# Even projection steps, Q ahead of the norm's rates, and K's and V's low weight halves on GpSimd, in a two-layer decoder step

## What is computed

```python
u = rmsnorm(h, mix_norm[0])                   # x * rsqrt(mean(x*x) + eps) * gain
q, k, v = split(u @ w_qkv, 3)                 # 8 heads, each with two sub-heads of 128; v has 256
o = (softmax1 - lam * softmax2) @ v           # causal, with linear biases; lam from four vectors
h = h + (rmsnorm(o) * (1 - lam0)) @ w_o       # norm over each head's 256
h = h + (silu(g) * up) @ w_down               # g, up from rmsnorm(h) @ w_gate_up
# layer 1: trailing-window means and w_pool in place of attention, then the same SwiGLU
```

## Time and profile before

| | |
|---|---|
| median of 3 runs | 3268.26 us (3264.95 to 3281.38) |
| profiled execution | 3269.89 us, its span 3268.1 us |
| TensorE busy | 3123.6 us, 96% of the span |
| TensorE weight loads, beside the matmuls | 2922.0 us, 89% |
| DVE busy | 1557.7 us, 48% |
| ACT busy | 1062.5 us, 33% |
| POOL busy | 159.4 us, 5% |
| read from HBM | 625.37 MB |
| start of the page steps, end of the last score | about 227 us, 1128 us |

### The profile page before, as it was taken

How to read it: one execution, slowest core, us unless ns; L and a number is a source line. 1 busy time by engine, 2 the same in 40 slices (tenths; PEclk the granted TensorE clock), 3 DMA queues, 4 the chain that set the end, 5 groups by cost and what they waited for, 6 DMA issues and landing times.

```text
span 3268.1 us, 59382 instructions
## 1 busy us (share of the span) xinstructions
PE 3123.6 (96%) x25401; PEld 2922.0 (89%) x25401; DVE 1557.7 (48%) x2212; ACT 1062.5 (33%) x1509; POOL 159.4 (5%) x185
## 2 busy tenths in 40 slices
PE   5899999999998899999999999999999999999999
PEld 5887777777775589999999999999999999999999
DVE  3244444444444455444444444445645445444445
ACT  3123333333333343322222222224432332323333
POOL 1000000000000011000000000002200000000002
PEclk8999999999999999999999999999999999999999
DMA  5438999999989955443444444443444444444442
GB/s 151 135 127 302 345 337 338 331 338 338 340 326 334 338 168 170 141 142 131 151 134 148 136 145 139 144 141 103 137 155 152 145 155 143 154 148 150 152 145 97
DMA packets 341938, 637.98 MB, mean 195 GB/s; under 512 B 11528, under 2 KB 257775, under 8 KB 308367
## 3 DMA queue, kind: packets, MB, share of 16 engines
q1 hardware_dynamic: 337120, 620.67, 54.7%
q0 software_dynamic: 3328, 11.24, 1.0%
q10 hardware_dynamic: 1230, 2.29, 0.2%
HBM read 625.37 MB, written 9.23 MB: 194 GB/s over the span
## 4 chain that ended last, share of the span: by engine, by line
PE 86%; DVE 6%; ACT 4%; issue 3%; DMA 1%; POOL 0%; ACTq 0%; DVEq 0%; SPq 0%
PE ps L1640 71%; PE ps L1754 6%; PE ps L1799 3%; PE ps L1776 2%; DVE halves L1087 2%; ACT kv_hi L836 1%; ACT halves L789 1%; DVE keyT L1257 1%; PE ps L1898 1%; DMA raw<-in_cache_k_dram 1%; PE ps L1878 1%; PE ps L1789 1%; PE ps L2041 1%; ACT pa_s L920 0%; PE ps L2018 0%
## 5 line engine op out<-in xcount | busy, mean ns | idle before, releaser
L1087 DVE TENSOR_TENSOR halves<-raw,halves 128x2048 fp32r<-128x2048 f32 x300 | 687.1, 2292 | 629.0 <-ACT halves L789 628.9
L1640 PE MATMUL ps<-xhi,halves 128*128 128x320 f32 (+1 forms) x3840 | 873.9, 314 | 33.9 <-DVE halves L1087 31.8
L789 ACT ACTIVATE halves<-raw 128x2048 fp32r<-128x2048 f32 x300 | 573.3, 1911 | 893.7 <-PE ps L1640 888.4
L1640 PEld LDWEIGHTS ps<-xhi,halves 128*128 128x128 f32 x3840 | 657.5, 190 | 37.1 <-issue 34.9
L1640 PE MATMUL ps<-yhi,halves 128*128 128x336 f32 x2816 | 657.2, 317 | 0.1
L1640 PE MATMUL ps<-xlo,halves 128*128 128x320 f32 (+1 forms) x1920 | 602.3, 314 | 0.0
L1640 PEld LDWEIGHTS ps<-yhi,halves 128*128 128x128 f32 x2816 | 483.1, 188 | 0.5 <-issue 0.4
L1640 PE MATMUL ps<-ylo,halves 128*128 128x336 f32 x1408 | 447.1, 318 | 0.0
L1640 PE MATMUL ps<-hA_hi,halves 128*128 128x336 f32 (+1 forms) x1408 | 375.5, 314 | 3.0 <-DVE hT L1531 2.9
L1640 PE MATMUL ps<-hB_hi,halves 128*128 128x336 f32 (+1 forms) x1408 | 372.8, 312 | 0.0
L1640 PEld LDWEIGHTS ps<-xlo,halves 128*128 128x128 f32 x1920 | 366.1, 191 | 0.1
(11 more groups left out here) (216 smaller groups left out, 2866.7 us busy)
## 6 DMA issues: line engine op xcount, KB each, us to landing
raw<-in_w_gate_up_dram SPq DMA_DIRECT2D x176, 1024.0 KB, 5.1
raw<-in_cache_k_dram SPq DMA_DIRECT2D x128, 1024.0 KB, 6.5
raw<-in_cache_v_dram SPq DMA_DIRECT2D x128, 1024.0 KB, 8.0
raw<-in_w_down_dram SPq DMA_DIRECT2D x88, 1024.0 KB, 5.0
kv_raw<-in_w_qkv_dram SPq DMA_DIRECT2D x64, 512.0 KB, 7.9
raw<-in_w_qkv_dram SPq DMA_DIRECT2D x16, 1024.0 KB, 5.9
raw<-in_w_o_dram SPq DMA_DIRECT2D x16, 1024.0 KB, 5.4
raw<-in_w_pool_dram SPq DMA_DIRECT2D x4, 1024.0 KB, 5.5
```

What stands on the lines that cost most here:

```text
L789: act.activation(whi[t][:, :], raw[r][:, :], ACT.Copy).then_inc(hi_ready[t], 1)
L1087: dve.tensor_tensor(wlo[t][:, :], raw[r][:, :], whi[t][:, :].bitcast(F32), ALU.subtract)\
L1640: mm = pe.matmul(out, l, r, start=first and n == 0, stop=last and n == 2)
```

## The change

A head's projection takes 16 steps: two chunks in each, eight steps for K and eight for V, and a block is turned in the step in which the next one begins. The tile's plan is tied to those 16 steps and its last phase has a step of its own. All chunks of the input are turned ahead of Q's first block. The sum of squares is taken on ACT from the rows as they came (six squares of 1024 columns with an accumulated sum), POOL raises it to the power of -1/2, DVE multiplies the identity by it, and three products with ones spread it over the partitions; the square root, the reciprocal and the Newton step are gone. Only the gain of the first norm is loaded ahead; the rest follows behind Q's first block. DVE's low half of unit n+1 stands ahead of the copy of the block that unit n ends. In the page steps the low halves of K's and V's weights are made on POOL, and ACT makes the high half right behind the key copies. The engines' order within a step is changed, the new keys take one step each from 114 on, and from key page 116 on there are two more page slots, where x's low and high halves stood. POOL loads x again at step 113.

The diff, cut (renamed banks, places and semaphores are left out):

```diff
@@ -59,9 +59,7 @@
 KV_RAW, KV_HI = 3, 2
-KV_STEPS = 15
-K_QUOTA = (3, 3, 2, 2, 2, 2, 2, 0)
-V_QUOTA = (3, 3, 3, 3, 2, 2, 0)
+KV_STEPS = 16
@@ -69,15 +67,11 @@
     for h in range(1, H):
-        t = KV_STEPS * (h - 1)
-        for block, quota in ((2 * h, K_QUOTA), (2 * h + 1, V_QUOTA)):
-            c = 0
-            for n in quota:
-                chunks[t] = [(block, c + i) for i in range(n)]
-                c += n
-                if n == 0:
-                    ends[t] = block
-                t += 1
+        for i in range(2):
+            t = KV_STEPS * (h - 1) + 8 * i
+            for n in range(8):
+                chunks[t + n] = [(2 * h + i, 2 * n), (2 * h + i, 2 * n + 1)]
+            ends[t + 8] = 2 * h + i
@@ -87,8 +81,8 @@
 NEW_SEQ = (7, 0, 1, 2, 3, 4, 5, 6)
-NEW_AT = {106 + 2 * n: n for n in range(NB)}
-PAIR_AT = {122 + 2 * p: p for p in range(3)}
+NEW_AT = {114 + n: n for n in range(NB)}
+PAIR_AT = {124 + 2 * p: p for p in range(3)}
@@ -118,14 +112,32 @@
 PAGE_ORDER = page_order()
-PAGE_LOAD = {what: n for n, what in enumerate(x for x in PAGE_ORDER if x[0] != "w")}
+IN_STEPS = [x for x in PAGE_ORDER if x[0] != "w"]
+PAGE_LOAD = {what: n for n, what in enumerate(IN_STEPS)}
+MORE_FROM = PAGE_LOAD["k", KV_STEPS * (H - 1) + 4]
+def page_slots():
+    last, turns, out = {i: None for i in range(4)}, {i: 0 for i in range(SLOTS)}, []
+    for n in range(len(IN_STEPS)):
+        if n == MORE_FROM:
+            last.update({4: None, 5: None})
+        slot = min(last, key=lambda i: -1 if last[i] is None else last[i])
+        out.append((slot, turns[slot], last[slot]))
+        last[slot], turns[slot] = n, turns[slot] + 1
+    return out
+PAGE_SLOT = page_slots()
...
 FREE_USES = [
-    ("in", {3: 1, 4: 5, 5: 5, 6: 4, 7: 4}),
+    ("in", {3: 2, 4: 5, 5: 5, 6: 4, 7: 4}),
...
     ("qg", {b: 4 for b in range(4)}),
-    ("hx", {4: 8, 5: 8}),
+    ("hx", {4: 16}),
@@ -608,17 +625,19 @@
                     continue
-                slot = n % SLOTS
-                if n < RAW:
-                    half_slot, half_turn = nth(U_Q + 12 + n, SPLIT)
+                slot, _, had = PAGE_SLOT[n]
+                if had is not None:
+                    page_used(had)
+                elif slot < RAW:
+                    half_slot, half_turn = nth(U_Q + 12 + slot, SPLIT)
...
                 else:
-                    page_used(n - SLOTS)
+                    sp.wait_ge(kv_used, 4 * KV_BLOCKS)
...
             for j in range(RAW):
-                page_used(max(n for n in range(len(in_steps)) if n % SLOTS == j))
+                page_used(max(n for n in range(len(IN_STEPS)) if PAGE_SLOT[n][0] == j))
@@ -666,12 +685,9 @@
-            for c in range(1, DC):
-                pool.wait_ge(squares, squares_n(0, c))
-                if c > 1:
-                    pool.wait_ge(sums, sums_n(0, c - 1))
-                pool.tensor_tensor(acc0[:, :], sq0[:, 0, :] if c == 1 else acc0[:, :], sq0[:, c, :], ALU.add)\
-                    .then_inc(sums, 1)
+            pool.wait_ge(ms0_step, 2)
+            pool.wait_ge(ones_set, 3)
+            pow_half(rt0[:, :], ms0[:, :], half[:, 0:3]).then_inc(rt0_set, 1)
@@ -694,15 +710,25 @@
+            def kv_split_lo(n):
+                pool.wait_ge(kv_split, n)
+                pool.wait_ge(kv_hi_set, n + 1)
+                pool.tensor_tensor(kv_lo[n % KV_RAW][:, :], kv_raw[n % KV_RAW][:, :],
+                                   kv_hi[n % KV_HI][:, :].bitcast(F32), ALU.subtract).then_inc(kv_split, 1)
...
             for t in range(STEPS + 2):
+                for n in range(9, 4 * KV_BLOCKS):
+                    if KV_FIRST[n - 1] == t:
+                        kv_split_lo(n)
...
                     pow_half(prs, pms, half[:, 0:1]).then_inc(pa_rs, 1)
-                if t - 1 in KV_END:
-                    block_rows(KV_END[t - 1])
+                if t in KV_END:
+                    block_rows(KV_END[t])
@@ -793,15 +819,22 @@
                 act.activation(xhi[:, c, :], ps[b][:, 0:T], ACT.Copy, scale=gain_of(0, c)).then_inc(norm_hi, 1)
-                act.activation(sq0[:, c, :], ps[b][:, 0:T], ACT.Square).then_inc(squares, 1)
...
                     split_hi(U_Q + 1)
+            act.wait_ge(ss0_clear, 1)
+            for part in range(2):
+                for tile in range(3):
+                    r = ROWS[tile]
+                    if part:
+                        act.wait_ge(ss0_set, tile + 1)
+                    act.activation(junk0[tile][0:r, :], io_tm[0:r, tile, 1024 * part:1024 * part + 1024], ACT.Square,
+                                   accum_out=ss0[0:r, part, tile:tile + 1]).then_inc(ss0_set, 1)
+            for n in range(2, 4):
+                split_hi(U_Q + n)
...
             act.activation(lsc[0:1, 2:4], lsc[0:1, 0:2], ACT.Exp).then_inc(lam_exp, 1)
-            act.wait_ge(bank_free[7], bank_n("n0", 7, 0) + 1)
-            act.activation(r0[:, :], mean0[:, :], ACT.Sqrt).then_inc(rms_ready, 1)
@@ -949,19 +982,23 @@
             for t in range(-1, STEPS):
-                if t - 1 in KV_END:
-                    kv_rows(KV_END[t - 1])
+                if t + 1 < PAGES:
+                    keys_out(t + 1, 0)
+                if tile_at(t, 4) is not None:
+                    tile_squares(tile_at(t, 4))
+                if t + 1 < PAGES:
+                    keys_out(t + 1, 2)
+                if t in KV_END:
+                    kv_rows(KV_END[t])
+                for n in range(9, 4 * KV_BLOCKS):
+                    if KV_FIRST[n - 1] == t:
+                        kv_split_hi(n)
...
                     tile_turned(tile_at(t, 3))
-                if tile_at(t, 4) is not None:
-                    tile_squares(tile_at(t, 4))
-                if tile_at(t - PHASES, 0) is not None:
-                    tile_features(tile_at(t - PHASES, 0))
+                if tile_at(t, 5) is not None:
+                    tile_features(tile_at(t, 5))
...
                     out_features(PAIR_AT[t - 2])
-                if t + 1 < PAGES:
-                    keys_out(t + 1, 0)
-                    keys_out(t + 1, 2)
@@ -973,9 +1010,6 @@
                     tile_exps(tile_at(t, 1))
-                for n in range(9, 4 * KV_BLOCKS):
-                    if KV_FIRST[n - 1] == t:
-                        kv_split_hi(n)
@@ -1088,13 +1122,13 @@
+            dve.memset(ss0[:, :, :], 0.0).then_inc(ss0_clear, 1)
             dve.wait_ge(bank_full[3], 1)
-            dve.tensor_scalar(gains[:, :], ps[3][:, 0:96], 1.0, None, ALU.mult).then_inc(bank_free[3], 1)
+            dve.tensor_scalar(gains[:, 0:16], ps[3][:, 0:16], 1.0, None, ALU.mult).then_inc(bank_free[3], 1)
...
                 dve.wait_ge(norm_hi, c + 1)
-                dve.wait_ge(squares, squares_n(0, c))
@@ -1103,6 +1137,21 @@
+            dve.wait_ge(ss0_set, 6)
+            dve.tensor_tensor(ms0[:, :], ss0[:, 0, :], ss0[:, 1, :], ALU.add).then_inc(ms0_step, 1)
+            dve.wait_ge(ms0_step, 1)
+            dve.tensor_scalar(ms0[:, :], ms0[:, :], 1.0 / D, 1e-6, ALU.mult, ALU.add).then_inc(ms0_step, 1)
+            dve.wait_ge(rt0_set, 1)
+            for tile in range(3):
+                dve.tensor_scalar(diag0[tile][:, :], ident, rt0[:, tile:tile + 1], None, ALU.mult).then_inc(diag_set, 1)
+            split_lo(U_Q + 2)
+            dve.wait_ge(bank_full[7], bank_n("n0", 7, 0, True))
+            dve.tensor_scalar(r0[:, :], ps[7][:, 0:T], 1.0, None, ALU.mult).then_inc(bank_free[7], 1)
+            dve.wait_ge(bank_free[7], bank_n("n0", 7, 0) + 1)
+            dve.wait_ge(bank_full[3], 2)
+            dve.tensor_scalar(gains[:, 16:96], ps[3][:, 0:80], 1.0, None, ALU.mult).then_inc(bank_free[3], 1)
+            split_lo(U_Q + 3)
@@ -1136,8 +1191,6 @@
-            rates("n0", mean0[:, :], r0[:, :], newton0[:, :], 0, 0)
@@ -1212,18 +1265,16 @@
-            dve.wait_ge(consts_in, 16)
-            dve.tensor_scalar(crow0, sel[:, 1:2], lam_b, None, ALU.mult).then_inc(sign_step, 1)
-            dve.wait_ge(sign_step, 1)
-            dve.tensor_tensor(rowsign, crow0, sel[:, 0:1], ALU.add).then_inc(sign_step, 1)
             for n in range(1, 16):
-                if n > 1:
-                    split_lo(U_Q + n)
-                if n == 15:
+                if 3 <= n < 15:
+                    split_lo(U_Q + n + 1)
+                elif n == 15:
...
                     q_evac(n)
+                if n == 5:
+                    lambdas()
@@ -1420,9 +1471,6 @@
                     tile_join(tile_at(t, 2))
-                for n in range(9, 4 * KV_BLOCKS):
-                    if KV_FIRST[n - 1] == t:
-                        kv_split_lo(n)
@@ -1670,31 +1718,33 @@
-            for c in range(4):
+            for c in range(DC):
                 turn_in(c)
-            def input_ready(cc):
-                if cc + 4 < DC:
-                    turn_in(cc + 4)
-                pe.wait_ge(*chunk_done(0, cc))
...
                 take("qg", e, 0)
-            fm_block(U_Q, 0, 0, (0, 1), input_ready, 0)
```

(60 more changed lines are left out.)

107 lines of the change are left out of this document (59 added, 48 removed).

## The result

The changed kernel takes 3189.84 us (median of 4 runs, 3186.87 to 3191.74) against 3267.91 us before (4 runs, 3264.95 to 3281.38): a ratio of 0.9752, 95% interval 0.9724 to 0.9781. The forecast was 3204 us. The profiled execution took 3186.87 us, 83.0 less than the one of before, where the sum had -64. So the total came out near, but two of its terms did not, and they were off in opposite directions; that they cancelled in part is luck.

A forecast was written before the change was run, and what follows sets the result against it. TensorE was taken as the nearer limit in the page steps, DMA close, with TensorE waiting for low halves in Q. 3269.9 - 44 - 16 + 8 - 12 = 3206, stated as 3204 for the median; range 3185 to 3222.

The forecast's parts named there:

- Part 1: Q ahead of the page steps: TensorE's pauses for low halves go and block 0 ends earlier, a gain of 44 us.
- Part 2: Page steps with a projection: a 16-step cycle takes 109.8 us; -16 us over seven cycles, between -35 and 0.
- The port term: Page steps: GpSimd's low halves hold VectorE instructions with two SBUF inputs through the shared port, +8 us, bounds 0 and +40.
- two or three meetings per cycle: Page steps: VectorE operations meeting GpSimd's low halves, half with DVE ahead, cost TensorE about 1.1 us per cycle.
- Part 3: Steps without a projection: -25.4 for seven plain steps and +13 for the last 15, so -12 us; bounds -18 and 0.
- No stall of some 19 us at the x loads: Sign of a right forecast: the 18.7 us for which loads of x for the residual shut the keys out would go.
- (a): Rival: DMA sets the page steps at 337 GB/s, a cycle takes 114.2 us, total 3227; chance 0.17.
- (b): Rival: slower, GpSimd's low halves hold DVE's queue and the key copy; 3317 at 2.2 us per half; chance 0.05.
- (c): Rival: evening buys nothing, parts 2 and 3 sum to 0 and Q alone gains: 3224; chance 0.15.
- (d): Rival: Q's pauses stay in half of the blocks, -22 and not -44, total 3226; chance 0.07.

The follow-up runs named there:

- added subtractions: The changed kernel with two more GpSimd subtractions of 128 x 448 behind each low half, into an area that nothing reads: 3206.86 us, ratio 0.9789.
- Q alone: The kernel before with only the Q part of the change; page steps, loads, x rows and low halves as before: 3231.52 us, ratio 0.9882.
- the spread from step 113 and the low halves on VectorE: The changed kernel with x loads in seven parts, one a step from step 113, and low halves back on VectorE: 3176.98 us, ratio 0.9696.

## Why the prediction was right, and where not

**Part 1, right.** -46.4 against -44, and about as much alone. Unit n+1 covers the halves of unit n+2, there is no pause, and the clock stays at its upper level. One step was off: block 0 was to run at the low clock from 26 to 43.5; it ran from 24.5 to 40.1 at 1.00, right behind the turning of all chunks.

**Part 2, the mechanism misread, and so a third of its size.** I forecast a cycle of 109.8 us, 110.9 with the port; it is 106.9. "The low half (1.23) now leaves DVE" gave 2.8 us per cycle, and "ACT's high half moves ahead" no term at all. The experiments turn this round. Steps 0 to 112, in us:

| steps | high half | low half | us |
|---|---|---|---|
| uneven, old order | late | VectorE | 804.0 (before) |
| uneven, old order | early | VectorE | 773.1 |
| even | late | VectorE | 787.7 |
| even | early | VectorE | 735.8 |
| even | late | GpSimd | 777.6 |
| uneven, new order | early | GpSimd | 782.8 |
| even | early | GpSimd | 740.7 (after) |

The rows with even steps hold the new order too. And the first two rows end with seven steps that the others don't have, with three of the new-key steps and the x loads in them: 54.8 and 53.3 us. A step with neither takes 4.8 us (step 105 of the kernel before). With seven such steps in their place, an estimate, the first two rows come to 783 and 753. Read so, the early high half alone brings 29 us, evenness with the new order alone brings nothing (787.7 against 783), and the two together 47. So the 63.3 us of the table are 21 for the moved loads and new keys (25.4 forecast), 47 for the early high half and the even steps with their order (16 forecast), less 4.9 for GpSimd. How much of the 47 is the order is not shown; in the new order, with GpSimd's queue in it, uneven steps cost 42 us. The early high half and the even steps need each other: an early high half wants a free buffer, which three chunks in a step don't leave, and even steps don't help while VectorE stands 3 us at a low half whose high half is late. The row for it was in my own group, 153.6 us of idle time before the low half, released by ScalarE's high half; I took the duration from it and left the wait.

**The port term, right in sign, smaller.** +8 predicted; with an early high half the move to GpSimd costs 4.9 (with a late one it brings 10.1). The forecast had two or three meetings per cycle, half of them with VectorE ahead. There are three, one with VectorE ahead. These are start, us, engine and line of one meeting of each kind:

```profile
448.62 0.49 DVE L1426 SCALAR_TENSOR_TENSOR pa_a<-pa_s,pa_n,pa_a 128x256 f32<-128x256 f32 x1
448.82 2.53 POOL L717 TENSOR_TENSOR kv_lo<-kv_raw,kv_hi 128x1024 fp32r<-128x1024 f32 x1 [11.99 <-ACT kv_hi L869]
...
474.68 2.39 POOL L717 TENSOR_TENSOR kv_lo<-kv_raw,kv_hi 128x1024 fp32r<-128x1024 f32 x1 [10.11 <-ACT kv_hi L869]
475.39 1.72 DVE L1414 TENSOR_SCALAR pa_n<-pa_n 128x2 f32<-128x2 f32 x1
```

A joining that starts ahead isn't held; the seven low halves behind one take 2.53 to 2.54 us, the others at most 2.39. The negated maximum starts behind a low half in 14 places, ends within 0.03 us of it in each, and takes 944 ns at the mean against 165. Behind it ScalarE's exponentials and then its key copies come late; made on ScalarE it gives back 1.7 of the 4.9 us, and the rest isn't shown. No padded query ran beside a low half. The other price of GpSimd is its queue: whatever is late there delays the tile's power.
Of the Trainium skill's rule (SBUF — State Buffer, "SBUF: two separate sides") I had weighed the half on two SBUF inputs. That page of the Trainium skill names a second case, VectorE operations in a two-port mode, and locks the pair for the whole instruction of whichever starts first. The trace agrees with the lock and the order (2.53 us behind a joining, 1.72 us behind a low half), and the key copies out of PSUM are not held. That the negated maximum, with one input and in SBUF alone, runs in such a mode no run here shows.

**Part 3, wrong.** "No stall of some 19 us at the x loads" was named as a sign; it is 25.6. I let the stall go with the plain steps, though the five loads are issued in one burst two steps behind the last chunk, much as before, and the page loads stand in the same DMA engines. The steps 112 to 127 were to cost +13, they cost +24.1; with the x rows spread from step 116 on, and the low halves on VectorE, +11. So the term left out the stall, and the rest of it was about right. The two slots, which I named as an offset, do nothing that can be told.

**The rivals.** (a) falls: the DMA engines deliver 355 GB/s over 740.7 us, so 337 was not all there is, and TensorE waits for no page there. (b) falls: the key copy takes 692 ns at the mean, with GpSimd's halves and without; but only 9 of 225 ran beside a half. With the added subtractions 69 ran beside GpSimd's work, and the mean is 691. (c) falls for the change as a whole: undoing evenness alone costs 42 us. But where both halves stay late it is what happens: that kernel has a ratio of 0.9874, Q alone 0.9882. (d) falls with the earlier trace rows's counterpart above.

The forecast held since -30 in steps 0 to 112 and +11 behind them were inside the range together. Open are why the clock falls in the page steps with the Q part alone, where 3.2 of GpSimd's 4.9 us arise, and why the spread from step 113 and the low halves on VectorE don't quite add up.

## What to carry to other kernels

Price an instruction with the idle time in front of it and its releaser: where a consumer stands in a queue and waits for a producer, moving the producer earlier can bring more than moving the consumer to another engine (52 us and 10 in this kernel with even steps). Before that, look whether the producer's buffers come free that early, for else it takes the stall into its own queue. A burst of loads that nobody needs for ten steps belongs behind the loads that are needed at once, a part per step.

## What was not expected of the hardware

An operation of two columns on VectorE took 0.92 to 1.72 us in the 14 places of steps 0 to 112 where GpSimd's 2.4 us subtraction ran beside it, and 0.17 in the other 7. The DMA engines kept 355 to 357 GB/s at a share of 0.94 to 0.95 for more than 700 us with TensorE waiting for no page.
